# The gate of the expert stage: one Silu on ScalarE in place of a tanh there and a product on VectorE

## The chip, the cores and the metric

One core of one Trainium2 chip runs the whole kernel as one launch. The metric is the device time of that launch in microseconds (us), lower is better. TensorE is PE in the profile, its weight loads are PEld, VectorE is DVE, ScalarE is ACT, GpSimd is POOL, and SyncE (SP) issues most transfers.

## The reference

Two model blocks run one after the other on 512 tokens of width 1024. The change concerns only the last part of the second block, its mixture of experts: 32 experts, 4 chosen for each token, and the token and expert pairs sorted into blocks of at most 128 rows, all of one expert.

```python
def clamped_swiglu(gu):
    glu, lin = jnp.split(gu, 2, axis=-1)
    glu = jnp.minimum(glu, SWIGLU_LIMIT)
    lin = jnp.clip(lin, -SWIGLU_LIMIT, SWIGLU_LIMIT)
    return glu * jax.nn.sigmoid(SWIGLU_ALPHA * glu) * (lin + 1.0)
...
    def expert_block(args):
        tok, g, e = args
        xb = h_pad[tok]
        gu = xb @ w_gate_up[e] + b_gate_up[e]
        y = clamped_swiglu(gu) @ w_down[e] + b_down[e]
        return y * g[:, None].astype(y.dtype)
```

`SWIGLU_LIMIT` is 7.0 and `SWIGLU_ALPHA` is 1.702. Everything is float32.

## The kernel before

The program has two stages that matter here. The first (to about 1265 us) computes the first model block, and attention, convolution and routing of the second. The expert stage fills the rest. It works on one block of 128 rows after another: `block_products` on TensorE, `block_highs` on ScalarE, `block_lows` on VectorE, `block_halves` on SP and `block_rows` on GpSimd, all written out by hand as fixed sequences, with semaphores between them. A hardware loop (`Fori`) runs two blocks a turn; the last two blocks stand behind it. With these inputs there are 32 blocks.

**Halves.** The weights of an expert are 6 tiles of 128x4096, and each comes in two halves of 128x2048 float32 (1 MB). A block so has 12 halves, named by their place `p` from 0 to 11 (`HALVES`). The table `TURN` gives what a place holds: gate and linear columns first, the down product (tiles 4 and 5) at p = 6, 7, 10 and 11, and at p = 8 and 9 already the first gate tile of the next block. Four halves run ahead of the blocks (`FIRST`), so place p of block b is half number `half_at(b, p)`.

**High and low parts.** A float32 product is made from three products of rounded parts. For each half ScalarE copies the raw weights to a rounded high part (`high_part`, L1393), VectorE subtracts this from the raw weights to get the low part (`low_part`, L1452), and TensorE does 12 matmuls with a free size of 512 (`half`, L1727): 8 with the high part of the weights, then 4 with the low part. There are 6 buffers for raw halves (`RAW`) and 4 for split ones (`SPLIT`). ScalarE may write split buffer n once TensorE has used half n - 4 (semaphore `used`); SP loads the next raw half into a buffer when VectorE has made the low part that was read from it (semaphore `low`).

**Activations.** The rows of a block (gathered by GpSimd) are transposed by TensorE (`turn_rows`, 8 matmuls, L1300), and split by ScalarE (`turned_high`, L1399) and VectorE (`turned_low`, L1458) into `rows_T`. The gate and linear products land in the four banks 0 to 3 of `ps`, in two groups of 512 hidden units, group 0 and group 1 (`at_`). For each group VectorE bounds the gate (`clipped_gate`, L1468), ScalarE takes tanh of half the scaled gate (L1426 for group 0 behind the high part of p = 1, L1435 for group 1 behind that of p = 7), and VectorE finishes in `hidden_rows` (before p = 5 for group 0, before p = 9 for group 1): it bounds the linear part (L1472), makes `(tanh + 1) * gate` (L1474), and, after a `drain`, `(lin + 1) *` this (L1476) into `hidden`. That is twice the wanted value, so the split of the transposed hidden rows scales it by 0.5. TensorE transposes `hidden` in two parts of 4 matmuls, and `hidden_T` is again split by L1399 and L1458.

**Where TensorE waits for this.** Two waits on `t_out` stand before products that read `hidden_T`: before p = 6 (the part made from group 0, `turned + 1`) and before p = 10 (the part made from group 1, `turned + 2`). On VectorE the L1458 that ends the first wait stands between the low parts of p = 7 and p = 8, and that which ends the second one stands behind the low part of p = 11.

Of the kernel before, what the change touches and what calls it, by code (L numbers as in the profile page):

```python
# [23 lines left out]
ALU = mybir.AluOpType  # L24
ACT = mybir.ActivationFunctionType
# [9 lines left out]
S = 512  # L35
# [193 lines left out]
def build(nc, io):  # L229
    ctx = ExitStack()  # L230
    with ctx:
# [70 lines left out]
        xg, y_sb = xgy[:, 0:2, :], xgy[:, 2:4, :]  # L302
        b_raw = scr[0:3 * E_N, 5 * D:8 * D]

        glu, thb, lin = (act_buf[:, i, :] for i in range(3))
        ps = ctx.enter_context(nc.psum_tensor("ps", [P, 8, 512], F32))

        def carve(at, *dims):
# [888 lines left out]
        used = sem("half_used")  # L1197
        t_full, t_high, t_out = sem("t_full"), sem("t_high"), sem("t_out")
        sel_ready = sem("sel_ready")
        glu_ready, th2_ready, act_ready = sem("glu_ready"), sem("tanh_ready"), sem("act_ready")  # L1200
        ye_ready, scattered = sem("ye_ready"), sem("scattered")
        acc_in, fin_ready, out_done, z_ready = sem("acc_in"), sem("fin_ready"), sem("out_done"), sem("z_ready")

# [184 lines left out]
        def experts_act(act):  # L1388
            n = block_pairs(act)

            def high_part(n_, p, landed_, earlier=0, raw_at=None):
                act.wait_ge(*landed_)
                nc.scalar.activation(wsp[:, (p - earlier) % SPLIT, 0], raw[:, p % RAW if raw_at is None else raw_at, :], ACT.Copy).then_inc(  # L1393
                    high, 3 if p == 1 else 1)

            def turned_high(dst, bank, wide, at, scale=1.0):
                act.wait_ge(t_full, at)
                src = ps[:, bank:bank + wide, :].rearrange("p a b -> p (a b)")
                nc.scalar.activation(dst, src, ACT.Copy, scale=scale).then_inc(t_high, 1)  # L1399

            def take_out(s):
                nc.scalar.activation(y_sb[:, s, :], ps[:, 4:6, :].rearrange("p a b -> p (a b)"), ACT.Copy,  # L1402
                                     scale=lst[:, s, 1:2].bitcast(F32)).then_inc(ye_ready, 1)

            act.wait_ge(CA.full, CA.n)
            act.wait_ge(CV.full, CV.done(0, "pos"))
            high_part(0, 0, (raw_in[2], 16), raw_at=2)
            act.wait_ge(CV.full, CV.done(0, "gates"))
            nc.scalar.activation(gate_T[0:3 * E_N, :], ps[0:3 * E_N, CV.bank("gates"), :], ACT.Copy).then_inc(gates_high, 1)
            high_part(1, 1, (raw_in[3], 16), raw_at=3)  # L1410
            for q in range(2):
                turned_high(xgT[:, 0, 0, q * S:(q + 1) * S], 6 + q, 1, q + 1)

            def block_highs(b, s, last=False):
                turned = 3 * b + (2 if last else 3)
                for p in range(HALVES):
                    if p == 8:
                        turned_high(hTe[:, 0, 0:S], 6, 1, turned + 1, 0.5)
                    if last and TURN[p][2]:
                        continue  # L1420
                    skipped = 2 if last and p > 9 else 0
                    act.wait_ge(used, half_at(b, p) - skipped - SPLIT + 1)
                    high_part(half_at(b, p) - skipped, FIRST + p, raw_landed(b, p), skipped)
                    if p == 1:
                        act.wait_ge(glu_ready, 2 * b + 1)
                        nc.scalar.activation(thb, glu, ACT.Tanh, scale=ALPHA / 2).then_inc(th2_ready, 1)  # L1426
                    if p == 3:
                        act.wait_ge(lst_ready, b + 1)
                        act.wait_ge(used, HALVES * b + FIRST)
                        take_out(1 - s)  # L1430
                    if p == 5 and not last:
                        turned_high(xgT[:, 1 - s, 0, :], 6, 2, turned)
                    if p == 7:
                        act.wait_ge(glu_ready, 2 * b + 2)
                        nc.scalar.activation(thb, glu, ACT.Tanh, scale=ALPHA / 2).then_inc(th2_ready, 1)  # L1435
                turned_high(hTe[:, 0, S:D], 7, 1, turned + 2, 0.5)

            with act.Fori(0, n) as i:
                for s in range(2):
                    block_highs(2 * i + s, s)  # L1440
            block_highs(2 * n, 0)
            block_highs(2 * n + 1, 1, last=True)
            act.wait_ge(lst_ready, 2 * n + 3)
            final_act(act, n)

        def experts_dve(dve):
            n = block_pairs(dve)

            def low_part(n_, p, earlier=0, raw_at=None):
                dve.wait_ge(high, n_ + 1)  # L1450
                at_ = (p - earlier) % SPLIT
                nc.vector.tensor_tensor(wsp[:, at_, 1], raw[:, p % RAW if raw_at is None else raw_at, :], wsp[:, at_, 0].bitcast(F32),  # L1452
                                        ALU.subtract).then_inc(low, 3 if p == 1 else 1)

            def turned_low(dst, high_, bank, wide, at, scale=1.0):
                dve.wait_ge(t_high, at)
                src = ps[:, bank:bank + wide, :].rearrange("p a b -> p (a b)")
                nc.vector.scalar_tensor_tensor(dst, src, scale, high_.bitcast(F32), ALU.mult,  # L1458
                                               ALU.subtract).then_inc(t_out, 1)

            def select(b, s):

                nc.vector.tensor_scalar(sel[:, s, :], be_bc[:, bass.ds(b, 1)].to_broadcast([P, P]),
                                        q_(par2, "part32"), None, ALU.is_equal).then_inc(sel_ready, 1)

            def clipped_gate(b, at_):
                dve.wait_ge(used, half_at(b, -3 if at_ == 0 else 3) + 1)
                nc.vector.tensor_scalar(glu, ps[:, 2 * at_, :], LIMIT, None, ALU.min).then_inc(glu_ready, 1)  # L1468

            def hidden_rows(b, at_):  # L1470
                dve.wait_ge(used, half_at(b, 1 if at_ == 0 else 5) + 1)
                nc.vector.tensor_scalar(lin, ps[:, 2 * at_ + 1, :], LIMIT, -LIMIT, ALU.min, ALU.max)  # L1472
                dve.wait_ge(th2_ready, 2 * b + at_ + 1)
                nc.vector.scalar_tensor_tensor(glu, thb, 1.0, glu, ALU.add, ALU.mult)  # L1474
                dve.drain()  # L1475
                nc.vector.scalar_tensor_tensor(h_sb[:, at_ * S:(at_ + 1) * S], lin, 1.0, glu, ALU.add,  # L1476
                                               ALU.mult).then_inc(act_ready, 1)
                dve.drain()

            dve.sem_inc(act_ready, 2)  # L1480
            nc.vector.memset(ps[:, 4:6, :], 0.0)
            select(0, 0)
            for p in range(2):
                low_part(p, p, raw_at=2 + p)
            for q in range(2):
                half_of = slice(q * S, (q + 1) * S)
                turned_low(xgT[:, 0, 1, half_of], xgT[:, 0, 0, half_of], 6 + q, 1, q + 1)

            def block_lows(b, s, last=False):
                turned = 3 * b + (2 if last else 3)  # L1490
                for p in range(HALVES):
                    skipped = 2 if last and p > 9 else 0
                    if p == 1:
                        clipped_gate(b, 0)
                    if p == 3 and not last:
                        select(b + 1, 1 - s)
                    if p == 5:
                        hidden_rows(b, 0)
                    if p == 6 and not last:
                        turned_low(xgT[:, 1 - s, 1, :], xgT[:, 1 - s, 0, :], 6, 2, turned)  # L1500
                    if p == 7:
                        clipped_gate(b, 1)
                    if p == 8:
                        turned_low(hTe[:, 1, 0:S], hTe[:, 0, 0:S], 6, 1, turned + 1, 0.5)
                    if p == 9 and not last or p == 11 and last:
                        hidden_rows(b, 1)
                    if p == 11 and last:
                        turned_low(hTe[:, 1, S:D], hTe[:, 0, S:D], 7, 1, turned + 2, 0.5)
                    if not (last and TURN[p][2]):
                        low_part(half_at(b, p) - skipped, FIRST + p, skipped)  # L1510
                if not last:
                    turned_low(hTe[:, 1, S:D], hTe[:, 0, S:D], 7, 1, turned + 2, 0.5)

            with dve.Fori(0, n) as i:
                for s in range(2):
                    block_lows(2 * i + s, s)
            block_lows(2 * n, 0)
            block_lows(2 * n + 1, 1, last=True)
            final_dve(dve, n)
# [1451 lines left out]
```

## Time and profile before

| | |
|---|---|
| median of 3 runs | 2465.73 us (2463.63 to 2466.58) |
| the profiled execution, its own time | 2464.16 us |
| its span in the profile | 2462.3 us |
| granted TensorE clock, mean over the span | 0.986 |
| PE busy | 2402.7 us, 98% |
| DVE busy | 2016.8 us, 82% |
| ACT busy | 1314.7 us, 53% |
| POOL busy | 665.1 us, 27% |

The profiled execution took 1.9 us more than its span and is 1.6 us below the median. A share of busy time is a mean over stages with different limits, so the expert stage has to be read by itself. A busy PE also does not mean a PE at its peak: a matmul counts from its start to its end, about 0.39 us, while the next one can start 0.23 us after it.

### The profile page before, as it was taken

To read this page: it belongs to the slowest core of one execution; us is meant where nothing else is said; L and a number is where in the kernel's file an instruction comes from. 1 tells how busy PE (TensorE), PEld (TensorE's weight loads), DVE (VectorE), ACT (ScalarE), POOL (GpSimd) and SP (SyncE) were. 2 spreads that over 40 slices of the span, in tenths; PEclk is the share of its full clock that TensorE was granted. 3 is DMA by queue.
4 is the path that set the end of the run, shared out by engine and by line. 5 is a ranking of instruction groups with operands and counts; after the bars stand their busy time and mean duration, and the time that the engine had idled before them with its cause. 6 is when DMAs were issued, how large, how long until landed. Compare 5 with 4: busy or idle time off the path is not lost.

```text
span 2462.3 us, 31625 instructions
## 1 busy us (share of the span) xinstructions
PE 2402.7 (98%) x10925; PEld 1932.1 (78%) x10925; DVE 2016.8 (82%) x1855; ACT 1314.7 (53%) x1207; POOL 665.1 (27%) x402
## 2 busy tenths in 40 slices
PE   8999999999999999999979999999999999999998
PEld 7677788777777887887868888888888888888887
DVE  7687568576875796887379999999999999999995
ACT  4342233334422234425357777777777777777773
POOL 5333251333423523342311112112112212211200
PEclk9999999999999998999989999999999999999998
DMA  6232246222422572331279999999999999999993
GB/s 241 86 115 82 64 138 218 64 82 69 137 69 77 207 280 62 103 94 35 88 229 360 370 374 369 366 377 364 366 369 372 367 368 374 367 364 375 367 361 128
DMA packets 105324, 572.41 MB, mean 232 GB/s; under 512 B 14921, under 2 KB 15081, under 8 KB 55402
## 3 DMA queue, kind: packets, MB, share of 16 engines
q1 hardware_dynamic: 87530, 513.46, 56.2%
q0 software_dynamic: 17424, 57.73, 8.4%
q8 instruction: 51, 0.84, 0.1%
q14 instruction: 31, 0.25, 0.0%
q10 hardware_dynamic: 288, 0.14, 0.0%
HBM read 558.68 MB, written 25.70 MB: 237 GB/s over the span
## 4 chain that ended last, share of the span: by engine, by line
PE 68%; DVE 17%; issue 7%; ACT 4%; DVEq 3%; DMA 1%; ACTq 0%; POOL 0%; POOLq 0%
PE ps L1727 67%; DVE w_split L1452 6%; ACT w_split L1393 3%; DVEq L1475 2%; DVE scr L2588 1%; DVE scr L2428 1%; DVE hidden_T L1458 1%; DVE act_buf L1468 1%; DVE hidden L1476 1%; DVE rows_T L1458 1%; DVE act_buf L1474 1%; DMA scr<-in_ada 1%; DVEq L2590 1%; DVE y_split L2365 1%; PE ps L1300 1%
## 5 line engine op out<-in xcount | busy, mean ns | idle before, releaser
L1452 DVE TENSOR_TENSOR w_split<-raw,w_split 128x2048 fp32r<-128x2048 f32 x384 | 873.0, 2287 | 57.5 <-ACT w_split L1393 46.2
L1727 PE MATMUL ps<-y_split,pieces_split 128*128 128x512 f32 x3600 | 845.9, 395 | 15.8 <-POOLq L2795 7.3
L1393 ACT ACTIVATE w_split<-raw 128x2048 fp32r<-128x2048 f32 x384 | 732.2, 1916 | 180.3 <-PE ps L1727 173.3
L1727 PEld LDWEIGHTS ps<-y_split,pieces_split 128*128 128x128 f32 x3600 | 679.9, 189 | 168.0 <-issue 26.0
L1727 PE MATMUL ps<-w_split,rows_T 128*128 128x512 f32 x3072 | 745.8, 393 | 1.0 <-DVE rows_T L1458 1.0
L1727 PEld LDWEIGHTS ps<-w_split,rows_T 128*128 128x128 f32 x3072 | 570.9, 188 | 117.6 <-DVE rows_T L1458 1.5
L2783 POOL TENSOR_TENSOR pieces_split<-pieces,pieces_split 128x1024 fp32r<-128x1024 f32 x151 | 372.0, 2474 | 648.4 <-ACT pieces_split L2061 518.7
L2061 ACT ACTIVATE pieces_split<-pieces 128x1024 fp32r<-128x1024 f32 x144 | 151.4, 1058 | 425.1 <-PE ps L1727 394.1
L1727 PE MATMUL ps<-w_split,hidden_T 128*128 128x512 f32 x1536 | 369.1, 396 | 8.6 <-DVE hidden_T L1458 6.3
L1727 PEld LDWEIGHTS ps<-w_split,hidden_T 128*128 128x128 f32 x1536 | 284.5, 188 | 92.7 <-DVE hidden_T L1458 35.0
L1538 POOL COPY rows_i<-slot_tokens 128x1 int32 x30 | 54.6, 1820 | 354.6 <-PE ps L1300 354.1
L1727 PE MATMUL ps<-scr 128*128 128x128 f32 (+3 forms) x576 | 137.6, 387 | 2.7 <-DVEq L1003 1.7
L1552 POOL DMA_INDIRECT acc_rows<-rows,lst x32 | 63.8, 1994 | 250.4 <-ACT rows L1402 250.4
L1727 PE MATMUL ps<-pieces_split,y_split 128*128 128x512 f32 (+1 forms) x672 | 126.1, 347 | 0.0
L1727 PEld LDWEIGHTS ps<-scr 128*128 128x128 f32 x576 | 86.7, 191 | 46.5 <-issue 33.6
L1727 PEld LDWEIGHTS ps<-pieces_split,y_split 128*128 128x128 f32 x672 | 106.7, 189 | 16.2 <-issue 1.4
L1543 POOL COPY lst<-slot_tokens 128x1 int32 (+1 forms) x33 | 10.2, 308 | 297.6 <-DMA acc_rows<-rows,lst 295.5
L1532 POOL DMA_INDIRECT rows<-h_rows,rows_i x30 | 81.3, 2711 | 25.2 <-issue 25.2
L2350 DVE RECIPROCAL scr<-scr 128x512 f32<-128x512 f32 (+1 forms) x20 | 63.9, 3193 | 24.8 <-ACT scr L2010 21.1
L2080 ACT ACTIVATE mix<-ps 128x512 f32<-128x512 f32 x32 | 19.0, 595 | 107.7 <-DVE ps L2404 107.7
L2588 DVE SCALAR_TENSOR_TENSOR scr<-scr,cond 128x1024 f32<-128x1024 f32 x56 | 70.6, 1281 | 5.6 <-DMA scr<-in_ada 3.1
L1399 ACT ACTIVATE hidden_T<-ps 128x512 fp32r<-128x512 f32 x64 | 37.7, 590 | 49.6 <-PE ps L1300 49.6
(299 smaller groups left out, 2077.5 us busy)
## 6 DMA issues: line engine op xcount, KB each, us to landing
raw<-in_w_moe SPq DMA_DIRECT2D x384, 1024.0 KB, 7.4
pieces<-in_pieces SPq DMA_DIRECT2D x181, 512.0 KB, 3.6
scr<-in_ada POOLq DMA_DIRECT2D x48, 512.0 KB, 5.5
scr<-in_ple SPq DMA_DIRECT2D x2, 1536.0 KB, 6.9
acc_rows<-in_zeros POOLq DMA_DIRECT2D x5, 512.0 KB, 11.0
h_rows<-shift_row SPq DMA_DIRECT2D x1, 2052.0 KB
hT<-in_xT SPq DMA_DIRECT2D x8, 256.0 KB, 5.1
h_rows<-scr POOLq DMA_DIRECT2D x4, 512.0 KB, 10.1
```

The source lines that it names most:

```text
L1393: nc.scalar.activation(wsp[:, (p - earlier) % SPLIT, 0], raw[:, p % RAW if raw_at is None else raw_at, :], ACT.Copy).then_inc(high, 3 if p ...
L1452: nc.vector.tensor_tensor(wsp[:, at_, 1], raw[:, p % RAW if raw_at is None else raw_at, :], wsp[:, at_, 0].bitcast(F32), ALU.subtract).the ...
L1458: nc.vector.scalar_tensor_tensor(dst, src, scale, high_.bitcast(F32), ALU.mult, ALU.subtract).then_inc(t_out, 1)
L1475: dve.drain()
L1532: nc.gpsimd.indirect_dma_start(out=xg[:, s, :], out_offset=None, in_=h2_dram[:, :], in_offset=bass.IndirectOffsetOnAxis(ap=index.bitcast(U ...
L1538: nc.gpsimd.tensor_copy(rows_i[:, s:s + 1], list_tok[:, bass.ds(b, 1)])
L1552: nc.gpsimd.indirect_dma_start(out=acc_dram[:, :], out_offset=bass.IndirectOffsetOnAxis(ap=lst[:, s, 0:1].bitcast(U32), axis=0), in_=y_sb[ ...
L1727: return pe.matmul(out, lhsT, rhs, start=start, stop=stop)
L2061: nc.scalar.activation(wps[:, n % A_SPLIT, 0], pieces[:, place_of(after, at_), :], ACT.Copy).then_inc(p_high, 1)
L2350: nc.vector.reciprocal(r, r)
L2588: last = nc.vector.scalar_tensor_tensor(out, aring[slot], c, out, ALU.mult, ALU.add)
L2783: nc.gpsimd.tensor_tensor(wps[:, n % A_SPLIT, 1], pieces[:, place_of(layer, at_), :], wps[:, n % A_SPLIT, 0].bitcast(F32), ALU.subtract).t ...
```

## The change

ScalarE computes Silu of 1.702 times the bounded gate, which is 1.702 times the gate and its sigmoid together, and writes it to `gated` (the third of `act_buf`'s buffers that held the tanh). VectorE's product L1474 goes away; the final product reads `gated`. The factor 1.702 is taken out again where 0.5 stood before, so that scale becomes 1/1.702. VectorE's wait for ScalarE moves from before the removed product to before the final one, and the `drain` now stands between the bound of the linear part and this wait. One Silu of a single column is added before the expert blocks.

```diff
+            def gated_rows(b, at_):
+
+                act.wait_ge(glu_ready, 2 * b + 1 + at_)
+                nc.scalar.activation(gated, glu, ACT.Silu, scale=ALPHA).then_inc(gated_ready, 1)
+
...
             high_part(1, 1, (raw_in[3], 16), raw_at=3)
+
+            nc.scalar.activation(small[:, 1:2], small[:, 0:1], ACT.Silu)
             for q in range(2):
                 turned_high(xgT[:, 0, 0, q * S:(q + 1) * S], 6 + q, 1, q + 1)
...
                     if p == 8:
-                        turned_high(hTe[:, 0, 0:S], 6, 1, turned + 1, 0.5)
+                        turned_high(hTe[:, 0, 0:S], 6, 1, turned + 1, 1.0 / ALPHA)
...
                     if p == 1:
-                        act.wait_ge(glu_ready, 2 * b + 1)
-                        nc.scalar.activation(thb, glu, ACT.Tanh, scale=ALPHA / 2).then_inc(th2_ready, 1)
+                        gated_rows(b, 0)
...
                     if p == 7:
-                        act.wait_ge(glu_ready, 2 * b + 2)
-                        nc.scalar.activation(thb, glu, ACT.Tanh, scale=ALPHA / 2).then_inc(th2_ready, 1)
+                        gated_rows(b, 1)
...
                 nc.vector.tensor_scalar(lin, ps[:, 2 * at_ + 1, :], LIMIT, -LIMIT, ALU.min, ALU.max)
-                dve.wait_ge(th2_ready, 2 * b + at_ + 1)
-                nc.vector.scalar_tensor_tensor(glu, thb, 1.0, glu, ALU.add, ALU.mult)
                 dve.drain()
-                nc.vector.scalar_tensor_tensor(h_sb[:, at_ * S:(at_ + 1) * S], lin, 1.0, glu, ALU.add,
+                dve.wait_ge(gated_ready, 2 * b + at_ + 1)
+                nc.vector.scalar_tensor_tensor(h_sb[:, at_ * S:(at_ + 1) * S], lin, 1.0, gated, ALU.add,
                                                ALU.mult).then_inc(act_ready, 1)
                 dve.drain()
```

On VectorE, inside the loop over blocks, this stood around group 0 of the hidden rows (p = 4 to p = 6), with the semaphore that a row waits for:

```order
L1452 TENSOR_TENSOR w_split<-raw,w_split 128x2048 [waits high_ready]
L1472 TENSOR_SCALAR act_buf<-ps 128x512 [waits half_used]
L1473 ISA
L1474 SCALAR_TENSOR_TENSOR act_buf<-act_buf 128x512 [waits tanh_ready]
L1476 SCALAR_TENSOR_TENSOR hidden<-act_buf 128x512
L1450 REGISTER_ALU
L1452 TENSOR_TENSOR w_split<-raw,w_split 128x2048 [waits high_ready]
```

and in the changed kernel, whose lines of this part have other numbers (L1457 is the low part, L1477 the bound of the linear part, L1480 the final product):

```order
L1457 TENSOR_TENSOR w_split<-raw,w_split 128x2048 [waits high_ready]
L1477 TENSOR_SCALAR act_buf<-ps 128x512 [waits half_used]
L1479 ISA
L1480 SCALAR_TENSOR_TENSOR hidden<-act_buf 128x512 [waits gated_ready]
L1455 REGISTER_ALU
L1457 TENSOR_TENSOR w_split<-raw,w_split 128x2048 [waits high_ready]
```

One instruction of 128x512 is gone, the wait for ScalarE stands one instruction later, and nothing else has moved; it is the same for group 1.

On ScalarE, just before the loop over blocks, this stood between the high part of the second half and the first transposed rows:

```order
L1393 ACTIVATE w_split<-raw 128x2048 [waits half_in2,cv_full,ca_full]
L1409 ACTIVATE gates_by_expert<-ps 96x512 [waits cv_full]
L1393 ACTIVATE w_split<-raw 128x2048 [waits half_in3]
L1399 ACTIVATE rows_T<-ps 128x512 [waits t_full] x2
L1438 UNCONDITIONAL_BRANCH
```

and now (the branch is the entry to the loop, L1414 is the former L1409):

```order
L1393 ACTIVATE w_split<-raw 128x2048 [waits half_in2,cv_full,ca_full]
L1414 ACTIVATE gates_by_expert<-ps 96x512 [waits cv_full]
L1393 ACTIVATE w_split<-raw 128x2048 [waits half_in3]
L1417 ACT_TABLE_LOAD
L1417 ACTIVATE small<-small 128x1
L1399 ACTIVATE rows_T<-ps 128x512 [waits t_full] x2
L1443 UNCONDITIONAL_BRANCH
```

A table load and a one-column Silu are added. From here to the end of the blocks neither kernel has another table load, and both have one before the square roots at the end.

## Rows read from the trace of the kernel before

**Rows 1.** The page: busy time, share of the span and instructions of each engine.
```profile
PE 2402.7 (98%) x10925; PEld 1932.1 (78%) x10925; DVE 2016.8 (82%) x1855; ACT 1314.7 (53%) x1207; POOL 665.1 (27%) x402
```

**Rows 2.** One block: length; busy PE, PEld, DVE, ACT, POOL; clock, DMA share, GB/s.
```profile
1704.85:1741.04 36.19, 36.02 (x165) 29.25 (x165) 34.46 (x25) 26.85 (x18) 7.04 (x5) 1.00 0.99 369
```

**Rows 3.** Waits, 1280 to 2425 us: in total, times, longest.
```profile
ACT w_split L1393 <- PE ps L1727: 165.6, 187, 2.8
...
PEld ps L1727 <- DVE hidden_T L1458: 35.0, 63, 2.6
...
PE ps L1727 <- DVE hidden_T L1458: 6.3, 18, 2.2
```

**Rows 4.** Timeline, PE: start, length, and in brackets the idle time before.
```profile
1717.21 5.60 PE L1727 MATMUL ps<-w_split,rows_T 128*128 128x512 f32 x24
...
1725.96 3.00 PE L1727 MATMUL ps<-w_split,rows_T 128*128 128x512 f32 x12
...
1729.12 5.74 PE L1727 MATMUL ps<-w_split,hidden_T 128*128 128x512 f32 x24 [0.15 <-DVE hidden_T L1458]
...
1738.00 3.02 PE L1727 MATMUL ps<-w_split,rows_T 128*128 128x512 f32 x12
...
1741.04 5.74 PE L1727 MATMUL ps<-w_split,hidden_T 128*128 128x512 f32 x24
```

**Rows 5.** Timeline, DVE and ACT, on the way to the wait before p = 6.
```profile
1713.66 1.92 ACT L1393 ACTIVATE w_split<-raw 128x2048 fp32r<-128x2048 f32 x1
...
1715.61 2.29 DVE L1452 TENSOR_TENSOR w_split<-raw,w_split 128x2048 fp32r<-128x2048 f32 x1 [0.74 <-ACT w_split L1393]
...
1717.82 0.68 DVE L1472 TENSOR_SCALAR act_buf<-ps 128x512 f32<-128x512 f32 x1
1718.42 0.68 DVE L1474 SCALAR_TENSOR_TENSOR act_buf<-act_buf 128x512 f32<-128x512 f32 x1
...
1719.17 0.69 DVE L1476 SCALAR_TENSOR_TENSOR hidden<-act_buf 128x512 f32<-128x512 f32 x1
...
1725.58 0.68 DVE L1468 TENSOR_SCALAR act_buf<-ps 128x512 f32<-128x512 f32 x1
...
1726.83 0.58 ACT L1399 ACTIVATE hidden_T<-ps 128x512 fp32r<-128x512 f32 x1
1727.31 3.71 ACT L1393 ACTIVATE w_split<-raw 128x2048 fp32r<-128x2048 f32 x2
1728.38 0.68 DVE L1458 SCALAR_TENSOR_TENSOR hidden_T<-ps,hidden_T 128x512 fp32r<-128x512 f32 x1
...
1729.25 2.29 DVE L1452 TENSOR_TENSOR w_split<-raw,w_split 128x2048 fp32r<-128x2048 f32 x1 [0.19 <-ACT w_split L1393]
```

**Rows 6.** Timeline, DVE, on the way to the wait before p = 10.
```profile
1731.46 0.68 DVE L1472 TENSOR_SCALAR act_buf<-ps 128x512 f32<-128x512 f32 x1
...
1733.68 6.70 DVE L1452 TENSOR_TENSOR w_split<-raw,w_split 128x2048 fp32r<-128x2048 f32 x3 [0.17 <-issue]
...
1740.30 0.68 DVE L1458 SCALAR_TENSOR_TENSOR hidden_T<-ps,hidden_T 128x512 fp32r<-128x512 f32 x1
```

**Rows 7.** Instructions on the tile act_buf: duration in ns, least, median, most.
```profile
L1474 DVE SCALAR_TENSOR_TENSOR act_buf<-act_buf x64: 679/681/683, 1282.9 to 2418.9; 128x512 f32<-128x512 f32 x64
...
L1426 ACT ACTIVATE act_buf<-act_buf x32: 632/633/635, 1273.0 to 2395.1; 128x512 f32<-128x512 f32 x32
```

**Rows 8.** DMA queues from 1290 to 2400 us, and the landing of the raw halves.
```profile
q1 hardware_dynamic: 52996, 385.93, 89.2%
q0 software_dynamic: 8506, 23.02, 8.9%
...
DMA to landing us min/median/max: 3.2/7.4/11.3
```

**Rows 9.** Timeline, ACT: a table load, and the last work before the blocks.
```profile
1239.94 1.28 ACT L937 ACT_TABLE_LOAD   x1
...
1261.17 0.60 ACT L1399 ACTIVATE rows_T<-ps 128x512 fp32r<-128x512 f32 x1 [4.42 <-PE ps L1300]
```

More of the change, by code:

```diff
@@ L303, in build @@
         b_raw = scr[0:3 * E_N, 5 * D:8 * D]
-        glu, thb, lin = (act_buf[:, i, :] for i in range(3))
+        glu, gated, lin = (act_buf[:, i, :] for i in range(3))
         ps = ctx.enter_context(nc.psum_tensor("ps", [P, 8, 512], F32))
@@ L1199, in build @@
         sel_ready = sem("sel_ready")
-        glu_ready, th2_ready, act_ready = sem("glu_ready"), sem("tanh_ready"), sem("act_ready")
+        glu_ready, gated_ready, act_ready = sem("glu_ready"), sem("gated_ready"), sem("act_ready")
         ye_ready, scattered = sem("ye_ready"), sem("scattered")
@@ L1433, in block_highs @@
                     if p == 7:
-                        act.wait_ge(glu_ready, 2 * b + 2)
-                        nc.scalar.activation(thb, glu, ACT.Tanh, scale=ALPHA / 2).then_inc(th2_ready, 1)
-                turned_high(hTe[:, 0, S:D], 7, 1, turned + 2, 0.5)
+                        gated_rows(b, 1)
+                turned_high(hTe[:, 0, S:D], 7, 1, turned + 2, 1.0 / ALPHA)
             with act.Fori(0, n) as i:
@@ L1503, in block_lows @@
                     if p == 8:
-                        turned_low(hTe[:, 1, 0:S], hTe[:, 0, 0:S], 6, 1, turned + 1, 0.5)
+                        turned_low(hTe[:, 1, 0:S], hTe[:, 0, 0:S], 6, 1, turned + 1, 1.0 / ALPHA)
                     if p == 9 and not last or p == 11 and last:
@@ L1507, in block_lows @@
                     if p == 11 and last:
-                        turned_low(hTe[:, 1, S:D], hTe[:, 0, S:D], 7, 1, turned + 2, 0.5)
+                        turned_low(hTe[:, 1, S:D], hTe[:, 0, S:D], 7, 1, turned + 2, 1.0 / ALPHA)
                     if not (last and TURN[p][2]):
@@ L1511, in block_lows @@
                 if not last:
-                    turned_low(hTe[:, 1, S:D], hTe[:, 0, S:D], 7, 1, turned + 2, 0.5)
+                    turned_low(hTe[:, 1, S:D], hTe[:, 0, S:D], 7, 1, turned + 2, 1.0 / ALPHA)
             with dve.Fori(0, n) as i:
```

## The prediction

> **What bounds the kernel now.** I read the page first: PE is busy for 98% of the span and DVE for 82% [rows 1]. Such shares are means over unlike stages, so the second view is the table of windows over one expert block. A block takes 36.19 us, PE is busy in 36.02 of them at a granted clock of 1.00, DVE in 34.46, ACT in 26.85, and the DMA engines in 0.99 of the time [rows 2]. Three resources look full. The third view, the waits, says which one is late: TensorE waits for nothing but `hidden_T`, 63 times by its weight loads, 35.0 us in total, and 6.3 us by its matmuls [rows 3]. Two waits in each of 32 blocks are 64, so it is these two, every block.
>
> The timeline gives their price. In an undisturbed stretch 24 matmuls take 5.60 us from the first start to the last end; less the 0.39 us of the last one this is 23 steps of 0.227 us [rows 4]. Before p = 6 the last matmul starts at 1725.96 + 3.00 - 0.39 = 1728.57 and the next one at 1729.12: 0.55 us in place of 0.23, so 0.32 us lost, and the 24 matmuls that follow take 5.74 in place of 5.60 us, 0.14 more, while the pipeline fills again. Together 0.46 us. Before p = 10 the last start is 1738.00 + 3.02 - 0.39 = 1740.63 and the next 1741.04: 0.18 us, and again 0.14, together 0.32 us [rows 4]. A block loses 0.78 us; without both waits it would take 36.19 - 0.78 = 35.41 us.
>
> Why is `hidden_T` late? Not for its own inputs. Its high part on ACT starts at 1726.83 and takes 0.58 us, but the L1458 on DVE starts only at 1728.38 [rows 5]: DVE has been in its queue of work since 1715.61, without a gap that a longer wait would leave. It begins that queue after a wait of 0.74 us for the high part of p = 4, which ACT started at 1713.66 when TensorE had freed a split buffer. So this start is pinned by TensorE's own progress, and all that DVE does between 1715.61 and 1729.06 counts. Before p = 10 it is the same: after the bound at 1731.46 come the hidden rows, three low parts without a pause from 1733.68, and then L1458 at 1740.30, whose end at 1740.98 releases TensorE at 1741.04 [rows 4, 6].
>
> **The change, part by part.**
>
> *The removed product.* L1474 runs 64 times at 0.68 us [rows 7], but such instructions overlap a little. What the queue loses is read from starts: the linear bound at 1717.82, L1474 at 1718.42, L1476 at 1719.17 [rows 5]. These are 0.60 and, with the drain, 0.75 us. Now the drain follows the bound, so the final product starts about 0.75 us after it: 0.60 us saved for each group, 1.20 us of DVE in a block.
>
> *The wait before p = 6.* With the start pinned at 1715.61, L1458 would end 0.60 us earlier, at 1728.46, and with the 0.06 us from that end to the matmul TensorE could start at 1728.52. It wants to at 1728.57 + 0.23 = 1728.80. The wait is gone with 0.28 us to spare: 0.46 us gained.
>
> *The wait before p = 10.* The low part of p = 8 starts at 1729.25 when ACT's high part arrives, which follows the gate of group 1 on ACT, which follows DVE's bound at 1725.58 [rows 5]. That bound comes 0.60 us earlier; the transposes that ACT's next step also needs are done 0.04 us before a start at 1726.25, so the low part of p = 8 starts 0.58 us earlier. The second removed product gives 0.60 more, so L1458 comes 1.18 us earlier, ready at 1739.86. TensorE, itself 0.46 us earlier by now, wants it at 1740.86 - 0.46 = 1740.40. That wait is gone too, with 0.54 us to spare: 0.32 us gained. The high parts of p = 10 and 11 follow TensorE by way of `used` and so move with it, some 0.5 us or more ahead of the low parts that need them.
>
> *DVE as the next bound.* Its busy time falls from 34.46 to about 33.3 us, under 35.41.
>
> *DMA.* Its work in a block is 89.2 + 8.9 = 98.1% of 36.19, or 35.5 us [rows 8]. This is the narrow place: TensorE at 35.41 us would want DMA 100% busy and 0.1 us more. But six raw buffers at 3.0 us a half give a cycle of 18 us, of which landing takes 7.4 us in the median and the stay until the low part is done about 4.3 (1713.66 to 1717.90 [rows 5]). Some 5 us of early arrival remain. 32 blocks times 0.1 us is 3 us, which this can absorb, if DMA's idle 2% do disappear once more loads are in flight. I charge 2 us for friction. The bounds: nothing, or a floor of 0.98 to 0.99 of 36.19, 35.5 to 35.8 us, in every block.
>
> *Silu in place of tanh.* No row shows a Silu. Below it cannot undercut the tanh by much, and a gain there would be hidden, because ACT idles 9 us in a block [rows 2]. The nearest row is the tanh of the same shape at 0.633 us [rows 7], and a plain copy of that shape takes 0.58 [rows 5]; I take 0.63. The page "ScalarE: Activation LUTs" of the Trainium skill, section "What ACT_TABLE_LOAD costs", says that ACTIVATE runs at one element a cycle and lane for every function; the tanh and copy rows agree. By its rule nothing would change in the sum.
>
> *The moved wait.* For group 0 ACT works behind p = 1 and is asked before p = 5, over three halves or 9 us later. For group 1 it is asked at about 1731.6 and done at 1726.4. Nothing is held up; were it, the low part of p = 9 would stand behind it and TensorE at p = 10 behind that.
>
> *The added load and one-column Silu.* A table load takes 1.28 us [rows 9], the Silu of one column some 0.2. They fall into ACT's idle 4.42 us before 1261.17, where it waits for TensorE [rows 9]. Cost nothing; without that cover 1.5 us once. The Trainium skill, "ScalarE: Activation LUTs", same section, puts a switch at 2.66 us with a drain; by that figure it would still fit into the gap. Its section "Table sets: the hidden batching unit" speaks against this change more strongly, since a function of another set costs a load at each switch; here the instruction order shows no load between Silu and the copies inside the loop, so I give it no chance of its own. *The new scale* 1/1.702 is an immediate like 0.5: nothing.
>
> **The sum.** The wait before p = 6 is lost in 31 blocks at 0.46 = 14.3 us. In the first block, where TensorE waits longer (the 2.2 us in [rows 3]), 0.6. The wait before p = 10 is regained in about 30 blocks at 0.32 = 9.6 us, since in the last block what TensorE waits for is the path from its own transposes, and in the first it loses little. That is 24.5 us; less 2 for DMA 22.5. The profiled execution of 2464.16 us would become 2441.7, and the median of 2465.73, which is 1.6 above it, 2443.2. I say 2443.
>
> **The rivals.**
>
> *DMA becomes the bound.* For it speaks the share of 0.98 to 0.99 in the expert stage [rows 2, 8], against it that ACT's high parts wait for TensorE, 165.6 us, and never for a landing [rows 3], and that 3.2 us are enough for one. With a floor of 35.5 to 35.8 us and no help from early arrival the gain is 0.4 to 0.7 us in 32 blocks, 12 to 22 us: 2444 to 2454, in the middle 2450. Chance 0.2.
>
> *Only one wait goes.* The margins are 0.28 and 0.54 us. If the drain behind the bound, with the wait now behind it, costs 0.3 us more than the 0.75 us I read, the first margin is used up; if 0.5 us more, most of the gain at p = 6 is. Then 9.6 to 14 us remain: 2452 to 2456. Chance 0.08.
>
> *No difference.* TensorE's waits are pinned elsewhere, by something that moves along with it. Against it is the continuous queue of DVE in [rows 5, 6]. Time 2465. Chance 0.06.
>
> *Silu is a long instruction (slower).* Its place is ACT's step for group 1, ahead of the high part of `hidden_T` and of p = 8 and 9. A Silu of d us moves these by d - 0.63. Up to about 1.2 us the margin of 0.54 covers it; each further tenth adds a tenth to the wait before p = 10, and at about 1.2 + 0.78 = 2.0 us, three times the tanh, the whole gain is gone. At 2.5 us it costs 0.5 us in 32 blocks, 16 us: 2482. Chance 0.04, as tanh and copy are so alike.
>
> **How the numbers follow.** My forecast has 0.62, DMA 0.2, one wait 0.08, no difference 0.06, Silu 0.04. The likeliest case alone spans 2440 (no DMA cost) to 2447. The range for 8 in 10 takes in the DMA case and part of the next: 2438 to 2455. Faster by over 0.2% (5 us, about what a measurement of this kernel can tell from no change) are the first three cases, 0.9; same 0.06; slower 0.04.
>
> **What would show it.** In the profile after: TensorE's waits for `hidden_T` fall from 63 to a few, a block takes 35.4 to 35.6 us, the 24 matmuls after p = 5 follow at 0.227 us, DVE waits longer for `w_split` from ACT, the DMA share goes to 0.99 or 1.00, Silu takes 0.63 us. I am wrong if ACT's L1393 begins to wait for DMA landings in many blocks (the DMA rival), if a wait of about 0.3 us before p = 6 stays (the drain), or if the Silu is clearly above 1 us.

## The result, and the profile after

The changed kernel takes 2441.2 us in the median of 4 runs (2440.56 to 2441.60), the kernel before 2465.32 us in the 4 runs beside and ahead of it. The ratio is 0.990, 95% interval 0.9885 to 0.992: 1.0% faster, 24.1 us. The profiled executions differ by 2462.3 - 2439.1 = 23.2 us of span, at the same mean granted clock, 0.986.

The page of the changed kernel, where lines 1727, 1468, 1472, 1476, 1452, 1458 and 1402 of before have become 1731, 1473, 1477, 1480, 1457, 1463 and 1407:

```profile
span 2439.1 us, 31563 instructions
...
PE 2385.0 (98%) x10925; PEld 1937.1 (79%) x10925; DVE 1978.2 (81%) x1791; ACT 1320.3 (54%) x1209; POOL 652.2 (27%) x402
...
PE 87%; DVE 7%; DVEq 2%; issue 1%; ACT 1%; DMA 1%; ACTq 0%; POOL 0%; POOLq 0%
```

Its shares hardly differ from those of [rows 1]; by them nothing has happened. DVE has 64 instructions less. The third line is the chain that ended last. It was 68% PE, 17% DVE and 7% issue before, and is now 87% PE.

The waits between 1280 and 2405 us, the view of [rows 3]: engine, line, whom it waited for, total, times, longest.

```profile
ACT w_split L1393 <- PE ps L1731: 159.0, 217, 2.8
...
DVE w_split L1457 <- ACT w_split L1393: 48.7, 127, 1.0
...
DVE hidden L1480 <- issue: 10.1, 64, 0.2
PEld ps L1731 <- DVE hidden_T L1463: 4.3, 2, 2.6
PE ps L1731 <- DVE hidden_T L1463: 3.6, 2, 2.2
...
ACT w_split L1393 <- DMA raw<-in_w_moe: 1.6, 1, 1.6
```

TensorE's weight loads waited 63 times for `hidden_T`; now it is twice, once in the first block and once in the last, where it waits for the path from its own transposes. DVE waits more often for ACT (127 times, 97 before), and ACT waits for a landing once in some 370 halves.

The timeline of one block, against [rows 4] to [rows 6]: start, length, idle time before.

```profile
1707.07 2.29 DVE L1457 TENSOR_TENSOR w_split<-raw,w_split 128x2048 fp32r<-128x2048 f32 x1 [0.64 <-ACT w_split L1393]
...
1709.28 0.68 DVE L1477 TENSOR_SCALAR act_buf<-ps 128x512 f32<-128x512 f32 x1
1710.12 0.69 DVE L1480 SCALAR_TENSOR_TENSOR hidden<-act_buf 128x512 f32<-128x512 f32 x1 [0.16 <-issue]
...
1717.45 3.02 PE L1731 MATMUL ps<-w_split,rows_T 128*128 128x512 f32 x12
...
1719.33 0.68 DVE L1463 SCALAR_TENSOR_TENSOR hidden_T<-ps,hidden_T 128x512 fp32r<-128x512 f32 x1
...
1720.20 2.29 DVE L1457 TENSOR_TENSOR w_split<-raw,w_split 128x2048 fp32r<-128x2048 f32 x1 [0.19 <-ACT w_split L1393]
1720.30 5.60 PE L1731 MATMUL ps<-w_split,hidden_T 128*128 128x512 f32 x24
...
1730.71 0.68 DVE L1463 SCALAR_TENSOR_TENSOR hidden_T<-ps,hidden_T 128x512 fp32r<-128x512 f32 x1
...
1731.88 5.60 PE L1731 MATMUL ps<-w_split,hidden_T 128*128 128x512 f32 x24
```

Both groups of 24 products with `hidden_T` take 5.60 us, the undisturbed length, where they took 5.74. Before p = 6, `hidden_T` is complete at 1720.01, with 0.06 us for the signal at 1720.07, and TensorE's matmuls start at 1720.30 by their own pace: 0.23 us to spare. Before p = 10 it is 1731.39 + 0.06 against 1731.88: 0.43 us.

These margins are counted to the first matmul. Its weight load needs `hidden_T` too, and starts 0.22 us ahead of it:

```profile
1720.08 5.40 PEld L1731 LDWEIGHTS ps<-w_split,hidden_T 128*128 128x128 f32 x24
```

Counted to this load, the margin before p = 6 is only 0.01 us. The padding experiment below shows what this is worth.

DMA from 1290 to 2380 us, in the place of [rows 8]: packets, MB and share by queue, and the landing of the raw halves.

```profile
q1 hardware_dynamic: 53158, 387.10, 90.2%
q0 software_dynamic: 8503, 23.01, 9.0%
```
```profile
DMA to landing us min/median/max: 4.9/7.2/10.3
```

The share rose from 98.1% to 99.2% and the median landing did not get longer (7.4 before, 7.2 now).

One row serves as the clock of the blocks from here on: `take_out` runs once a block, so its first and last start, divided by 31, give the mean length of a block. Before, the first is at 1277.1 and the last at 2400.0:

```profile
L1402 ACT ACTIVATE rows<-ps,lst x32: 1092/1097/1102, 1277.1 to 2400.0; 128x1024 f32<-128x1024 f32 x32
```

and after:

```profile
L1407 ACT ACTIVATE rows<-ps,lst x32: 1092/1099/1102, 1277.4 to 2377.1; 128x1024 f32<-128x1024 f32 x32
```

That is 36.22 and 35.47 us, 0.75 us in each of 31 blocks, 23.2 us: the whole difference of the spans.

This mean holds one interval that is unlike the others, the first: 37.25 us before and 36.72 after. From the second `take_out` to the last, over 30 blocks, the lengths are 36.19 and 35.43 us, again 0.75 apart. Below, "block" is the mean of all 31 intervals and "steady block" that of these 30; where a few hundredths of a us count, the steady block is the one to read.

### The profile page after: what moved, and what is told of

It is laid out like the page before. It is cut to its first block, busy times and chain, and to the rows that moved or that the text cites. A ratio compares the mean times of both kernels' runs of the same rounds, so it can differ in the third digit from the quotient of the medians.

```text
span 2439.1 us, 31563 instructions
## 1 busy us (share of the span) xinstructions
PE 2385.0 (98%) x10925; PEld 1937.1 (79%) x10925; DVE 1978.2 (81%) x1791; ACT 1320.3 (54%) x1209; POOL 652.2 (27%) x402
## 4 chain that ended last, share of the span: by engine, by line
PE 87%; DVE 7%; DVEq 2%; issue 1%; ACT 1%; DMA 1%; ACTq 0%; POOL 0%; POOLq 0%
PE ps L1731 84%; PE ps L1300 2%; DVE scr L2592 1%; DVE scr L2432 1%; DVEq L2594 1%; DMA scr<-in_ada 1%; DVE y_split L2369 1%; PE ps L698 0%; DVE mix L2483 0%; DVE w_split L1457 0%; DVE scr L2481 0%; DVEq L2379 0%; DVE hT L2629 0%; DVE scr L1009 0%; ACT pieces_split L2065 0%
## 5 line engine op out<-in xcount | busy, mean ns | idle before, releaser
L1457 DVE TENSOR_TENSOR w_split<-raw,w_split 128x2048 fp32r<-128x2048 f32 x384 | 873.2, 2288 | 65.6 <-ACT w_split L1393 55.1
L1731 PE MATMUL ps<-w_split,hidden_T 128*128 128x512 f32 x1536 | 360.6, 391 | 3.6 <-DVE hidden_T L1463 3.6
L1547 POOL COPY lst<-slot_tokens 128x1 int32 (+1 forms) x33 | 60.5, 1833 | 297.2 <-DMA acc_rows<-rows,lst 295.5
L1542 POOL COPY rows_i<-slot_tokens 128x1 int32 x30 | 37.6, 1254 | 290.8 <-PE ps L1300 290.2
L1404 ACT ACTIVATE act_buf<-act_buf 128x512 f32<-128x512 f32 x64 | 40.5, 633 | 56.3 <-DVE act_buf L1473 56.3
```

What stands on the lines that cost most here:

```text
L1404: nc.scalar.activation(gated, glu, ACT.Silu, scale=ALPHA).then_inc(gated_ready, 1)
L1547: nc.gpsimd.tensor_copy(lst[:, s, 0:1], list_tok[:, bass.ds(b, 1)])
L1731: return pe.matmul(out, lhsT, rhs, start=start, stop=stop)
```

## The experiments

Each ran beside the kernel before, whose median was 2464.9 us in the first two sets (15 and 13 runs) and 2465.9 in the last (7 runs).

**The product back.** Silu and its scale stay; an unused product returns to the place of the removed one, and the wait and the `drain` return to their old places around it.

```diff
                 nc.vector.tensor_scalar(lin, ps[:, 2 * at_ + 1, :], LIMIT, -LIMIT, ALU.min, ALU.max)
-                dve.drain()
                 dve.wait_ge(gated_ready, 2 * b + at_ + 1)
+                nc.vector.scalar_tensor_tensor(glu, gated, 1.0, glu, ALU.add, ALU.mult)
+                dve.drain()
```

> The changed kernel (2441 us) with Silu as it is, but with one unused VectorE product of 128x512 where the removed one stood, and the wait and the drain in their old places around it. Theory (the gain is 0.5 to 0.6 us of VectorE queue in each group of hidden rows): the time goes back to 2465 us, within 2, a block back to 36.18 us, TensorE waits again 63 times for hidden_T. Rival (the gain comes from Silu on ScalarE, from the drain's new place or from the wait's): it stays at 2441.

Measured: 2465.45 us, ratio 1.0001 (0.9992 to 1.001). The block is back at 36.22 us, and so are the waits of TensorE:

```profile
PEld ps L1732 <- DVE hidden_T L1463: 34.9, 63, 2.6
```

One instruction of 0.68 us in each of VectorE's two stretches, with the old places of wait and `drain`, is worth the full 24 us. That the new places of these two brought part of the gain can be excluded from the rows: without a product between them, bound and final product start 0.84 us apart in the changed kernel, while the same `drain` behind the old product took 0.75 us from start to start. The new places cost a little.

**Tanh without the product.** The opposite edit, made to the kernel before: no Silu, no added table load, but the product gone too and the `drain` in its new place. The gate's factor is then missing from the output.

```diff
-                dve.wait_ge(th2_ready, 2 * b + at_ + 1)
-                nc.vector.scalar_tensor_tensor(glu, thb, 1.0, glu, ALU.add, ALU.mult)
                 dve.drain()
-                nc.vector.scalar_tensor_tensor(h_sb[:, at_ * S:(at_ + 1) * S], lin, 1.0, glu, ALU.add,
+                dve.wait_ge(th2_ready, 2 * b + at_ + 1)
+                nc.vector.scalar_tensor_tensor(h_sb[:, at_ * S:(at_ + 1) * S], lin, 1.0, thb, ALU.add,
```

> The kernel before with its tanh, no Silu and no added table load, but with the product L1474 left out and the drain in its new place; the gate's factor is missing from the output. Theory: 2441 us, the same as the changed kernel within 1 us, so that Silu, its table load and the new scale cost nothing. Rival (Silu brings part of the gain): between 2445 and 2465. Rival (the table load costs something): 1 to 2 us under the changed kernel.

Measured: 2441.36 us, block 35.48 us, which is the changed kernel. Silu only makes it possible to leave the product out; as an instruction it costs what the tanh costs.

**Group 0 alone, and group 1 alone.** In one kernel only group 0 has the change, in the other only group 1.

```diff
-                nc.scalar.activation(gated, glu, ACT.Silu, scale=ALPHA).then_inc(gated_ready, 1)
+                if at_ == 0:
+                    nc.scalar.activation(gated, glu, ACT.Silu, scale=ALPHA).then_inc(gated_ready, 1)
+                else:
+                    nc.scalar.activation(gated, glu, ACT.Tanh, scale=ALPHA / 2).then_inc(gated_ready, 1)
```

This is the kernel for group 0; the other tests for `at_ == 1`. `hidden_rows` and the scales of the split branch in the same way.

> The change for group 0 alone; group 1 keeps the tanh, the product and the scale 0.5. Theory (each wait is pinned by its own stretch of VectorE's queue): the wait before p = 6 goes, 0.46 us; before p = 10 VectorE comes 0.50 us earlier but TensorE also 0.46, so that wait stays almost whole. Gain 0.50 us in 31 blocks, 15.5 us: 2450. Rival (VectorE's total time counts, so each product is worth half of the 24 us): 2453. Second rival: nothing before both are gone, 2465.

> The change for group 1 alone; group 0 keeps the tanh, the product and the scale 0.5. Theory: the wait before p = 6 stays whole, since its queue holds the product of group 0; the one before p = 10 goes, 0.32 us in 30 blocks, 9.6 us: 2456. Rival (VectorE's total time): 2453. The two gains of this and of the kernel for group 0 alone should add up to 24 to 25 us.

Measured: group 0 alone 2448.2 us, ratio 0.9931 (0.9918 to 0.9945), block 35.72; group 1 alone 2454.6 us, ratio 0.9957 (0.9943 to 0.9971), block 35.90. In blocks these are 0.50 and 0.32 us, the theory's figures; equal halves of 0.375 are excluded. The waits show that one of the two stays. With group 0 alone:

```profile
PEld ps L1741 <- DVE hidden_T L1466: 15.0, 32, 2.6
PE ps L1741 <- DVE hidden_T L1466: 3.6, 2, 2.2
```

and with group 1 alone:

```profile
PEld ps L1741 <- DVE hidden_T L1466: 21.3, 33, 2.6
PE ps L1741 <- DVE hidden_T L1466: 6.0, 17, 2.2
```

About one wait a block remains in each, and the timeline says which. With group 0 alone the 24 products of p = 6 take 5.60 us, and those of p = 10 are the disturbed ones; with group 1 alone it is the other way round. The first line is from the kernel for group 0 (p = 10), the second from that for group 1 (p = 6):

```profile
1734.01 5.76 PE L1741 MATMUL ps<-w_split,hidden_T 128*128 128x512 f32 x24
1726.07 5.73 PE L1741 MATMUL ps<-w_split,hidden_T 128*128 128x512 f32 x24 [0.15 <-DVE hidden_T L1466]
```

The two gains add up to 0.82 us, more than the 0.75 of both together, because the product of group 0 also stands ahead of the second wait: its removal shortens a wait that the removal of the other one then takes away as well. In the mean of 28 blocks of the timeline (between 1330 and 2330 us) the wait before p = 10 costs 0.32 us in the kernel before and 0.25 us with group 0 alone, and these 0.07 us are the excess.

**A longer Silu.** An additional Silu into an unused buffer, ahead of that of group 1 (`at_` 1), of 128x512 and then of 128x1024.

```diff
+                if at_ == 1:
+                    nc.scalar.activation(spare[:, 0:S], glu, ACT.Silu, scale=ALPHA)
                 nc.scalar.activation(gated, glu, ACT.Silu, scale=ALPHA).then_inc(gated_ready, 1)
```

> The changed kernel (2441 us) with one more Silu of 128x512 into an unused buffer ahead of the Silu of group 1, as if that one took 0.53 us longer. It delays ScalarE's high part of p = 8, for which VectorE waits, by 0.53 us. In the profile after, the hidden_T for p = 10 is ready 0.43 us before TensorE wants it, so the theory (a margin of 0.43 us) gives a wait of 0.10 us and 0.14 for the refill in some 31 blocks: 7 us, 2448. Rival (ScalarE is off the path, it idles 9 us in a block): 2441. Rival (there is no margin and each delay counts whole): 0.53 x 31, 2458.

> As the kernel before it, but with 128x1024 more, 0.96 us. Theory: 0.96 - 0.43 = 0.53 us of wait before p = 10 and 0.14 for the refill, 0.67 in 31 blocks, 21 us: 2462, so that a Silu two and a half times as long as it is would have eaten nearly the whole gain. Rival (ScalarE off the path): 2441. Rival (each delay counts whole): 2471.

Measured: 2448.7 us, block 35.71, and 2461.2 us, block 36.11. Their steady blocks, 35.67 and 36.09, lie 0.24 us (0.24 expected) and 0.66 us (0.67 expected) above the 35.43 of the changed kernel. With the first, the low part of p = 8 starts 0.5 us later against TensorE, after a longer wait for ACT than the 0.19 us of the changed kernel, and the wait before p = 10 is back (DVE and PEld of one block):

```profile
1725.75 2.29 DVE L1459 TENSOR_TENSOR w_split<-raw,w_split 128x2048 fp32r<-128x2048 f32 x1 [0.71 <-ACT w_split L1393]
...
1737.00 1.00 PEld L1733 LDWEIGHTS ps<-w_split,hidden_T 128*128 128x128 f32 x5 [0.32 <-DVE hidden_T L1465]
```

So ScalarE, which idles for some 9 us of a block, is still on this path, with a margin of 0.43 us. The rival of the slow Silu had its mechanism right; it did not occur, since Silu takes 0.63 us. Its prices were too low: it let a Silu of about 1.2 us pass free, while 0.63 + 0.53 = 1.16 us already costs 0.24 us a block. It counted a margin of 0.54 us where there are 0.43, and left out the 0.14 us of the refill.

**Padding VectorE.** One unused instruction ahead of the final product of group 0, 128 columns wide and then 384.

```diff
                 dve.wait_ge(gated_ready, 2 * b + at_ + 1)
+                if at_ == 0:
+                    nc.vector.tensor_scalar(glu[:, 0:384], lin[:, 0:384], LIMIT, -LIMIT, ALU.min, ALU.max)
```

> The changed kernel with one unused VectorE instruction of 128x128 (0.20 us from start to start) before the final product of group 0. In the profile after, hidden_T for p = 6 is ready 0.23 us before TensorE wants it. Theory (VectorE's queue has this margin and no more): 0.20 fits, 2441 to 2442, no wait before p = 6. Rival (the margin is wrong, TensorE needs it earlier than the row's end shows): 2445 or more.

> As the kernel before it, but with 128x384, about 0.47 us from start to start. Theory: 0.47 - 0.23 = 0.24 us of wait before p = 6 and 0.14 for the refill, 0.38 in 31 blocks, 12 us: 2453. Nothing is added before p = 10, where TensorE then comes later too. Rival (no sharp edge, only VectorE's busy share counts, still under TensorE's): 2441.

Measured: 2445.2 us and 2446.8 us. By time alone the first speaks for the rival. The mean of all 31 intervals seems to speak against it:

```profile
L1407 ACT ACTIVATE rows<-ps,lst x32: 1092/1096/1105, 1280.2 to 2379.8; 128x1024 f32<-128x1024 f32 x32
```

This block is 35.47 us, as without the pad, but the equality is an accident of the first interval, 35.28 us here and 36.72 in the changed kernel. The steady block is 35.48 us, 0.04 above 35.43, and a block of the timeline shows where it comes from (PEld and PE before p = 6):

```profile
1722.02 5.30 PEld L1733 LDWEIGHTS ps<-w_split,hidden_T 128*128 128x128 f32 x24 [0.16 <-DVE hidden_T L1463]
1722.13 5.62 PE L1733 MATMUL ps<-w_split,hidden_T 128*128 128x512 f32 x24
```

The weight loads wait for `hidden_T` in every block (32 times, twice in the changed kernel), 0.18 us in the mean of 29 blocks. The first matmul still comes in time, 0.23 us after the one before it, but the 24 take 5.66 us in the mean (5.62 to 5.71), against 5.61 in the changed kernel. So the rival was right that TensorE needs `hidden_T` earlier than the margin of 0.23 us says, and it is worth 0.04 us a block, 1.3 us of the time. The other 3.1 us by which this execution's span is longer (2443.5 against 2439.1) lie outside: the second `take_out` comes 1.4 us later, and from the last to the end of the span it takes 63.7 us against 62.0. Why these edges differ stays open. All four runs of this kernel (2443.2 to 2446.7) are slower than all of the changed one, but only one has a trace.

The second has a steady block of 35.62 us, 0.19 above the changed kernel, where 0.38 was expected. The instruction was mis-sized:

```profile
1712.07 0.36 DVE L1481 TENSOR_SCALAR act_buf<-act_buf 128x384 f32<-128x384 f32 x1 [0.16 <-issue]
1712.35 0.69 DVE L1482 SCALAR_TENSOR_TENSOR hidden<-act_buf 128x512 f32<-128x512 f32 x1
```

It occupies VectorE for 0.28 us, not 0.47, and the 128 columns of the first pad for 0.14, not 0.20 (1711.95 to 1712.09). With 0.28, an excess of 0.28 - 0.23 = 0.05 us and 0.14 for the refill make 0.19. Three points describe the edge: a queue longer by 0, 0.14 and 0.28 us costs 0, 0.04 and 0.19 us a block. It is steep around the margin, but the cost begins before the margin is used up.

**What is next: without the biases.** TensorE loses four matmuls of a block; then VectorE also loses its bound of the linear part. The first kernel leaves out the biases of the gate and linear products, the second also that bound.

```diff
-                begins = j >= 4 and q == 0
+                begins = q == 0
...
-                bias(1, s)
...
-                nc.vector.tensor_scalar(lin, ps[:, 2 * at_ + 1, :], LIMIT, -LIMIT, ALU.min, ALU.max)
-                dve.drain()
```

> The changed kernel (2441 us, a block of 35.43) without the four bias matmuls of a block, which leaves the biases of the gate and linear products out: TensorE has 0.91 us less in a block. Three theories of what is next. DMA is the wall, its work of 0.99 x 35.43 = 35.1 us is fixed: a block of 35.1, 2431, with ScalarE waiting for landings. VectorE's queue is next (my theory): two of the four stand between the pinned start and p = 6, whose margin of 0.23 us becomes -0.22; a wait of 0.22 and a refill of 0.14 come back, a block of 34.9, 2424. Nothing is next: 34.5, 2412.

> As the kernel before it, and in addition without VectorE's bound of the linear part and the drain behind it (0.84 us in each group; the final product reads PSUM itself), so that VectorE can't be late. It leaves out the biases and that bound. If DMA's work is fixed: 35.1 us a block, 2431, with ScalarE waiting for landings. If its share counts more than work (my theory, since ScalarE's halves still land some 4 to 5 us early in the profile after): 34.5 us a block, 2412, at a DMA share that cannot go over 1.00.

Measured: 2425.9 us, steady block 34.93, with TensorE's waits for `hidden_T` back at 41 times; and 2410.9 us, steady block 34.55, with 2 such waits. In the second kernel the queues' shares from 1290 to 2350 us are:

```profile
q1 hardware_dynamic: 53129, 386.91, 91.6%
q0 software_dynamic: 8544, 23.13, 9.3%
```
```profile
DMA to landing us min/median/max: 5.7/7.3/10.1
```

The block came down to TensorE's own time (35.43 - 0.91 = 34.52 expected, 34.55 measured). The DMA shares add up to 100.9%, which the expectation had called impossible, and still a raw half lands 7.3 us after its issue. The wall that a share of 0.98 seemed to announce is not there down to 34.5 us. What held the first kernel at 34.93 was VectorE's queue: 0.50 us gained, of 0.91, where 0.53 was forecast. In the mean of 28 blocks, 0.38 us are lost before p = 6, where 0.36 was forecast, and 0.03 us, not forecast, before p = 10, where the matmuls come in time and the 24 products take 5.63 us, as with the small pad. The weight loads of two places in one block, p = 6 and p = 10:

```profile
1713.35 5.32 PEld L1726 LDWEIGHTS ps<-w_split,hidden_T 128*128 128x128 f32 x24 [0.48 <-DVE hidden_T L1458]
1724.74 5.33 PEld L1726 LDWEIGHTS ps<-w_split,hidden_T 128*128 128x128 f32 x24 [0.16 <-DVE hidden_T L1458]
```

## Why the prediction was right, and where its sizes were off

**The path** was right: VectorE's queue, not its inputs, made `hidden_T` late. The unused product in the place of the removed one, with wait and `drain` around it as before, brought the whole 24 us back, and the tanh kernel without it had the whole gain.

**Two waits with prices of their own** were right: 0.46 and 0.32 us were predicted, 0.78 together. Measured are 0.75 for both, 0.50 and 0.32 for each group alone. The prices were read from one block; in the mean of 28 blocks before, the first matmul of p = 6 starts 0.52 us after the one ahead of it, not 0.55, so that wait costs 0.44. The 0.50 of group 0 alone is this and the 0.07 by which the second wait shrinks.

**The removed product** was sized at 0.60 us a group, with the final product 0.75 us after the bound. It comes 0.84 us after it (1709.28 to 1710.12), so 0.51 us are saved. The row of after says `0.16 <-issue` there; that the wait, which now stands behind the drain, makes the 0.09 us was not tried. This is in the direction of the margins, which are 0.23 and 0.43 us and not 0.28 and 0.54, though 0.09 and twice 0.09 would leave 0.19 and 0.36. It cost no time: both stayed above zero, and no weight load waited in 29 blocks, though before p = 6 with 0.01 us to spare. That the loads need `hidden_T` 0.22 us before the matmuls is a term the prediction doesn't have; here this was luck.

**VectorE is not the next bound by its total, but is by its queue.** "Its busy time falls to about 33.3 us" holds: 1022.21 us in 1090 are 33.3 in 35.47. But the kernel without biases shows that it becomes the next limit at once, since 0.23 us of margin is all there is before p = 6.

**DMA** is the term that was wrong. The prediction took 98.1% of a block for work, 35.5 us, and charged 2 us of friction because TensorE wanted 35.41. No row shows such friction, and ScalarE waited for a single landing, 1.6 us. The share went to 99.2% of 35.47, which is 35.2, and in the last experiment to 100.9% of 34.55, 34.9 us. What the share counts is not a fixed amount of work. The bytes are the same (12 halves of 1 MB), so 34.5 us is an upper bound for the time they need, and the true floor was not reached here. The sum without that term is 2465.7 - 24.5 = 2441.2, the measured median, but such a hit is partly luck: the spans of the profiled executions differ by 23.2 us, not 24.5, and the times alone could not tell 22.5 from 24.5. A slip in the account of early arrival had no effect: 18 - 7.4 - 4.3 leaves 6.3 us, not 5. The rival in which DMA becomes the bound, with a chance of 0.2, fell with it.

**Silu, its load and its scale** cost nothing, as predicted. Silu takes 0.632 us where the tanh took 0.633:

```profile
L1404 ACT ACTIVATE act_buf<-act_buf x64: 631/632/636, 1273.3 to 2389.3; 128x512 f32<-128x512 f32 x64
```

The table load and the one-column Silu lie in ScalarE's idle time before the blocks, which fell from 4.42 to 2.92 us:

```profile
1257.01 1.28 ACT L1417 ACT_TABLE_LOAD   x1
1258.30 0.20 ACT L1417 ACTIVATE small<-small 128x1 f32<-128x1 f32 x1
1261.43 0.60 ACT L1399 ACTIVATE rows_T<-ps 128x512 fp32r<-128x512 f32 x1 [2.92 <-PE ps L1300]
```

The page "ScalarE: Activation LUTs" of the Trainium skill states in "What ACT_TABLE_LOAD costs" about 1283 ns for the load and about as much again for a drain. The load agrees; a drain does not appear, as the load starts 0.02 us after the ACTIVATE before it ended (1255.09 + 1.90 = 1256.99), and the next instruction 1.29 us after the load did.

## What to carry to other kernels

An engine that is busy for 82% of the span (34.46 of 36.19 us in a block, as VectorE), or idle for a quarter of a block (as ScalarE), can still set the pace: look for the point at which its queue is pinned to the bottleneck, add up what stands between that point and the release, and compare with the time the bottleneck spends between the same two points. What is taken out of such a stretch pays only until the margin turns positive, and what is put in costs little until it turns negative, then its excess and a refill at once. Count the margin to the first thing on the bottleneck that needs the data: here that was the weight load, not the matmul.

A DMA share near 1 in a loop with many transfers in flight does not say that DMA is the limit. Ask whether anything waits for data to land: at 98%, at 99% and at 101% no high part did, but one. And where two versions differ by a few us, compare the length of the repeated block, without the first one, and not only the total: from the second on, the intervals of the changed kernel are 35.41 to 35.45 us, while the first intervals of these kernels range from 34.06 to 37.29.

## What the runs showed of the hardware that was not expected

- A VectorE instruction from SBUF to SBUF with immediates (TENSOR_SCALAR 128x384) takes 0.36 us and lets the next one start after 0.28, and the same operation reading PSUM takes 0.68 us for 128x512. By columns that is 0.7 against 1.2 ns from start to start (0.28/384, 0.60/512), and between the two pads 256 more columns took 0.14 us more, 0.5 ns each. The Trainium skill has a rule that bears on it: "VectorE: DVE Perf Modes", section "Mode 2×_2P — use both read ports for one tensor", states that such an operation may use both read ports when it has a single tensor operand, in SBUF, at two results a cycle even for fp32. The rows agree in direction, but that the ports are the cause was not tried apart; the pads were sized from the PSUM row, without this rule.
- After a wait that delays its first matmul, TensorE's next 24 matmuls take 5.73 to 5.78 us in place of 5.60. This 0.14 us came with each such wait and went with it, in both directions.
- A weight load starts 0.22 us ahead of its matmul and can wait by itself: 0.18 us of such waiting with the small pad delayed no first matmul, and made the 24 take 5.66 us.
- The DMA share can exceed 1: 91.6 + 9.3 = 100.9% over 1060 us.
